# The last residual add moved from the vector engine into accumulating transfers to the output

## The reference, cut to what matters

```python
def sandwich_update(x, y_mix, mod, g, w1, w2):
    x = x + mod[2] * rmsnorm(y_mix, g[1])
    h = modulate(rmsnorm(x, g[2]), mod[3], mod[4])
    return x + mod[5] * rmsnorm(sq_relu_mlp(h, w1, w2), g[3])
```

## Time and profile before

| what | value |
| --- | --- |
| median of 3 runs | 1409.69 us (1409.33 to 2283.79) |
| the profiled execution's own time | 1409.05 us |
| its span, first to last instruction | 1407.0 us |
| PE busy | 1365.7 us (97%) |
| DVE busy | 889.8 us (63%) |
| ACT busy | 607.8 us (43%) |
| POOL busy | 123.1 us (9%) |
| DRAM read, written | 164.49 MB, 10.49 MB |

### The profile page before, as it was taken

One profiled execution on the slowest core, in us unless ns is written; L12 is line 12 of the kernel. 1 busy time (PEld: TensorE's weight loads), 2 busy tenths in 40 slices (PEclk: granted clock), 3 DMA queues, 4 the chain that ended last, 5 costly groups with the idle time before them and its releaser, 6 DMA issues. The chain is left out here.

```text
span 1407.0 us, 18116 instructions
## 1 busy us (share of the span) xinstructions
PE 1365.7 (97%) x6676; PEld 1123.4 (80%) x6676; DVE 889.8 (63%) x1279; ACT 607.8 (43%) x903; POOL 123.1 (9%) x151
## 2 busy tenths in 40 slices
PE   9989998999999999999998999999999999999996
PEld 2568787988888888888878888888888888888885
DVE  6898779977765555555457799998274333333333
ACT  3655446664462432514445344434446143251441
POOL 1761120002000000000110000000200000000011
PEclk9999999999999999999999999999999999999997
DMA  9534251119266565665221232230303233233221
GB/s 360 219 147 170 82 169 47 46 46 326 78 214 205 182 208 179 198 202 174 97 90 61 75 105 71 95 120 31 120 31 113 97 94 101 92 102 103 91 75 60
DMA packets 48331, 178.47 MB, mean 127 GB/s; under 512 B 5929, under 2 KB 6249, under 8 KB 45835
## 3 DMA queue, kind: packets, MB, share of 16 engines
q1 hardware_dynamic: 45194, 164.51, 34.4%
q0 software_dynamic: 3072, 13.11, 2.9%
HBM read 164.49 MB, written 10.49 MB: 124 GB/s over the span
## 5 line engine op out<-in xcount | busy, mean ns | idle before, releaser
L1758 PE MATMUL bank<-hhi,whi 128*128 128x512 f32 (+1 forms) x1000 | 377.3, 377 | 0.6 <-DVE wlo L1126 0.4
L1760 PE MATMUL bank<-hhi,wlo 128*128 128x512 f32 (+1 forms) x1000 | 374.4, 374 | 0.0
L1759 PE MATMUL bank<-hlo,whi 128*128 128x512 f32 (+1 forms) x1000 | 374.4, 374 | 0.0
L695 ACT ACTIVATE whi<-raw 128x1024 fp32r<-128x1024 f32 x180 | 189.1, 1053 | 231.6 <-PE bank L1760 199.9
L1126 DVE TENSOR_TENSOR wlo<-raw,whi 128x1024 fp32r<-128x1024 f32 x180 | 222.4, 1237 | 92.7 <-ACT whi L695 91.1
L1758 PEld LDWEIGHTS bank<-hhi,whi 128*128 128x128 f32 x1000 | 188.7, 189 | 34.4 <-issue 1.4
L1760 PEld LDWEIGHTS bank<-hhi,wlo 128*128 128x128 f32 x1000 | 188.6, 189 | 34.0
L1759 PEld LDWEIGHTS bank<-hlo,whi 128*128 128x128 f32 x1000 | 188.7, 189 | 32.8
L1760 PE MATMUL bank<-ghi,wlo 128*128 128x512 f32 x512 | 199.2, 389 | 0.0
L1758 PE MATMUL bank<-ghi,whi 128*128 128x512 f32 x512 | 199.2, 389 | 0.0
L1759 PE MATMUL bank<-glo,whi 128*128 128x512 f32 x512 | 199.2, 389 | 0.0
(11 more groups left out here) (275 smaller groups left out, 1963.8 us busy)
## 6 DMA issues: line engine op xcount, KB each, us to landing
raw<-in_wpack SPq DMA_DIRECT2D x180, 512.0 KB, 3.5
araw<-in_apack SPq DMA_DIRECT2D x40, 512.0 KB, 3.5
amore<-in_apack SPq DMA_DIRECT2D x36, 512.0 KB, 3.5
ablk<-in_ahead SPq DMA_DIRECT2D x8, 1024.0 KB, 12.3
spectra<-scratch SPq DMA_DIRECT2D x16, 512.0 KB, 2.9
araw<-spectra POOLq DMA_DIRECT2D x8, 1024.0 KB, 5.1
fs<-in_fw SPq DMA_DIRECT2D x2, 1024.0 KB, 11.2
x<-in_xT SPq DMA_DIRECT2D x1, 2048.0 KB, 14.6
```

The costliest lines, as they stand in the source:

```text
L695: A(whi[:, s, :], raw[:, r, :], ACT.Copy).then_inc(hi_done, 1)
L1758: mm(o, lh, rh, start=first, stop=False)
L1759: mm(o, lh, rl, start=False, stop=False)
L1760: return mm(o, ll, rh, start=False, stop=last)
```

## The change

Boundary 3 on DVE loses its four additions and keeps the four multiplications. SP writes the eight blocks of `x` to the output during the last MLP, between two weight loads, under a new semaphore `x_base`. POOL, after its last sum of squares, waits for `x_base`, then for each `scaled_done`, and issues two transfers a group from `y` to the output that add to what lies there (`accum_op=ALU.add`). SP's last waits are for both semaphores.

```diff
@@ -573,11 +574,12 @@
             load_quarter(QUARTERS - 1, ADA_ROWS - ADA_RING - ADA_OUT - (QUARTERS - 1) * ADA_QUARTER)
-            load_units(U_HY + 5, UNITS)
-            for i in range(X_GROUPS):
-                sp.wait_ge(x_done, 3 * X_GROUPS + i + 1)
-                for j in range(2 * i, 2 * i + 2):
-                    sp.dma_start(out[j], x[:, j, :]).then_inc(x_out, 16)
+            load_units(U_HY + 5, UNITS - 6)
+            sp.wait_ge(x_done, 3 * X_GROUPS)
+            for j in range(KC):
+                sp.dma_start(out[j], x[:, j, :]).then_inc(x_base, 16)
+            load_units(UNITS - 6, UNITS)
+            sp.wait_ge(x_base, KC * 16)
             for n in range(2):
                 sp.wait_ge(filt_out[n], 8 * 16)
             sp.wait_ge(x_out, KC * 16)
@@ -680,6 +682,11 @@
             y_sums(2)
             y_sums(3)
+            pool.wait_ge(x_base, KC * 16)
+            for i in range(X_GROUPS):
+                pool.wait_ge(scaled_done, 3 * X_GROUPS + i + 1)
+                for j in range(2 * i, 2 * i + 2):
+                    pool.dma_start(out[j], y[:, j, :], accum_op=ALU.add).then_inc(x_out, 16)
 
@@ -1497,8 +1504,6 @@
                         rows = B3[:, :].unsqueeze(1).broadcast_to([P, 2, NT])
                         TT(y[:, js, :], y[:, js, :], rows, ALU.mult).then_inc(scaled_done, 1)
-                        dve.wait_ge(scaled_done, X_GROUPS * b + i + 1)
-                        TT(x[:, js, :], x[:, js, :], y[:, js, :], ALU.add).then_inc(x_done, 1)
                     return
```

More of the change, by code:

```diff
@@ L203, in build @@
         x_out = sem("x_out")
+        x_base = sem("x_base")
         hi_done = sem("hi_done")
```

## The result

The changed kernel takes 1416.55 us (median of 6 runs, 1415.39 to 1417.19). Its ratio to the kernel before is 1.0046, 95% interval 1.0036 to 1.0056: slower by 6.5 us, 5 to 8. That is far inside the 2% that were called no change, and clear all the same. The one run of before at 2283.79 us is not in the ratio. The forecast was 1411, with a range of 1404 to 1428.

A forecast was written before the change was run, and what follows sets the result against it. The end was taken as bound by DVE, then one landing. Dropping four additions gains 5.0 us, but adding transfers at half the copy rate lose 6.6, net +1.6 over the profiled 1409.05; as a median 1411, range 1404 to 1428.

The forecast's parts named there:

- narrower range of the mechanism that was forecast: Whole kernel: time 1408 to 1416 from varied data start, read rate and issue cost; the forecast mechanism had chance 0.37.
- sign for giving the forecast up: End of the span: the forecast falls if it moves by more than 7 us.
- The loss: Whole kernel: net 1.6 us over the profiled time, from 5.0 us gained on DVE and 6.6 us lost in transfers.
- DVE's 5.0 us: Boundary 3 on DVE: without its four additions it ends 5.0 us earlier, at 1398.8 instead of 1403.81.
- The rate of adding: Final output transfers: adding fetches two operands per byte stored, so 4.19 MB at 385 GB/s take 10.9 us.
- The stretch of the data: Final adding transfers: data move from 1396.8 for 10.9 us, until 1407.7.
- The end behind the last byte: End of the kernel: the span ends 0.9 us after the last data, at 1408.6.
- SP's writes at zero: Early writes of x between loads 173 and 174: eight issues take 3.1 us in a 5.5 us gap, cost zero.
- adding as cheap as copying: Final transfers: adding costs no more than copying, data end at 1402.2, time 1405.2 profiled, 1405.8 as median; chance 0.22.
- Rows one after another: Final transfers: each row fetched, added and stored before the next, 86 us in series, time 1486; chance 0.09.
- DVE holding POOL's issues off: End of boundary 3: POOL cannot issue until DVE's multiplications end at 1398.8, time 1414; chance 0.03.
- The rival of 1.5 to 3 us a transfer: Final transfers: each adding one costs 1.5 to 3 us in listing or moving, time 1412 to 1424; chance 0.27.

The follow-up runs named there:

- e6_merged: Changed kernel with one adding transfer of 512 KB for each group instead of two of 256 KB; 1415.74 us, ratio 1.0047 to the kernel before.
- e2_pool_out: Kernel before with its last eight plain output transfers issued by POOL instead of SP; 1413.08 us, ratio 1.0014.
- e7_pool_last: Kernel before plus one 128 x 1 POOL multiplication behind DVE's last addition, which nobody waits for; 1411.6 us, ratio 1.0014.
- e1_copy: Changed kernel with its eight adding transfers turned into plain copies, so the output lacks x; 1410.02 us, ratio 0.9997 to the kernel before.
- e5_pool_adds: Kernel before, but POOL's own tensor_tensor adds groups 0 and 1 and DVE only groups 2 and 3; 1408.38 us, ratio 0.9988.
- e8_pool_three: Kernel before, but POOL's own arithmetic adds chunks 0 to 2 during DVE's scalings and DVE adds the rest; 1409.21 us, ratio 0.9992.
- e4_one_group: Changed kernel with adding transfers for group 0 only; DVE adds and SP writes groups 1 to 3; 1408.94 us, ratio 0.9994 to the kernel before.
- e9_mix: Kernel before, but group 0 goes by adding transfers, POOL's arithmetic adds group 1, DVE groups 2 and 3; 1409.12 us, ratio 0.9996.
- e3_base: Kernel before plus only SP's eight early writes of x between the loads of units 173 and 174; 1410.18 us, ratio 0.9998.

## Why the prediction was right, and where it was not

The direction was right and the range of 1404 to 1428 held the time. But the narrower range of the mechanism that was forecast, 1408 to 1416, did not hold the median of 1416.55. The wide range reached that far because of a rival whose mechanism is not there, so that it held the time is in part luck. The sign for giving the forecast up, an end of the span moved by more than 7 us, was missed narrowly: it moved by 6.6. The loss was put at 1.6 us against the profiled time and was 6.3 (1415.39 - 1409.05). By its steps:

- **DVE's 5.0 us**: right. Scalings 1.14 us apart, DVE done at 1399.0 against 1398.8, and 0.24 us of that is the shift ahead.
- **The rate of adding**: right, and it was the heart of the sum. 192 GB/s was taken, half of copying; the windows show about 200 once the stretch is under way, and swapping the adding for copying gives 6.8 us back. The Trainium skill, "Collectives: The Full Stack", section "The bandwidth ceiling: the fold count and why AG ≠ RS ≠ AR", has a reduction between cores move at half the rate of a copy. This trace agrees for an adding transfer on one core: 178 ns for an adding row of 2 KB, 172 ns for 4 KB of a copy.
- **The stretch of the data**: mis-sized. The sum had full rate from 1396.8 to the last byte. In fact the first issue came 0.55 us after POOL was released, each list took 0.89 us instead of 0.53, and the last byte was moved at 1410.45 instead of 1407.7, which is 2.5 us late when the shift is taken off. Against 192 GB/s, bytes worth 1.3 us are lacking by 1399 (the windows of 33 and 100 GB/s), 0.6 more from 1399 to 1402, and 0.8 at the end, where the engines' share falls to 0.59 and 0.12; the full rate in between makes 0.2 good. e6_merged shows that the lists as such are not the pace: with shorter lists the landing comes only 0.5 us sooner. What slows the first rows, and why the engines end unevenly, stays open.
- **The end behind the last byte**: this is the step that failed. The sum took the 0.9 us of before from the earlier trace rows as a constant. It is 3.2 us, and e2_pool_out and e7_pool_last show why: POOL closes its program 4.5 us or more after its last work, and 2.3 us or more after its last landing. Before, POOL had been idle since 1386, and that it was idle was listed only as a readiness, never as a cover that the change takes away.
- **SP's writes at zero**: right, though SP's issues cost 5.4 us and not 3.1.
- **The rivals**: adding as cheap as copying is refuted by e1_copy. Rows one after another is refuted by the rate. DVE holding POOL's issues off did not happen: they started 0.54 us apart throughout the scalings. The rival of 1.5 to 3 us a transfer would give this time, and its mechanism is not there: a list takes 0.89 us and does not set the pace, and to move a transfer takes about 1.3 us (0.26 MB at 200 GB/s).

Together: 2.5 us in the data and 2.3 behind the last byte, plus the shift of 0.2, less 0.3 because span and time lay 1.8 us apart in this execution and not 2.05. That makes 4.7, the difference between 1.6 and 6.3.

## What to carry to other kernels

An addition moved into the transfers is not free: where the engines are already full, it doubles the time of the bytes, and it belongs in a stretch with time to spare, never behind the last instruction. Ask of each engine what it does in the last 5 us: an engine that has long been idle has closed its program in cover, and any work given to it there, however small, brings that close to the end. And when the end is bound by one engine, another engine's own arithmetic can take part of its work: POOL's additions gave the only gain whose interval keeps clear of zero (1.7 us, 0.4 to 3.0). That this is more than adding transfers for one group can give (0.8 us, -0.4 to 2.1) is not shown, as the intervals overlap.

## What the runs showed of the hardware

- POOL's program is closed 4.5 us or more after its last instruction in all twelve executions, and 2.3 us or more after the last landing of a transfer of its own; a 0.19 us instruction at the end cost 2 us of span (e7_pool_last).
- POOL's list for an adding transfer costs 0.90 us for 128 rows and 1.26 for 256, where a plain one of 128 rows took 0.54 (e1_copy).
- POOL's and DVE's additions slow each other (2.35 to 3.33 us, 1.22 to 2.13), but POOL's addition beside DVE's scalings, which read one operand from PSUM, ran at 2.36 us, and the scalings kept their pace (4.61 us for four, as without POOL). The Trainium skill, "SBUF — State Buffer", section "Who interferes with whom", says that a DVE instruction with two inputs in SBUF (the on-chip memory that holds x and y) contends with a POOL instruction that reads there, and that one with at most one such input, outside the two-port modes, does not. e5_pool_adds and e8_pool_three agree.
- Plain issues of SP, mostly 0.33 to 0.44 us, took up to 1.04 us beside adding transfers of POOL (e4_one_group) and 1.12 just behind them (e9_mix). But they took up to 1.21 us in e3_base as well, which has no adding transfer, among its eight early writes issued one after another. So the adding transfers are not shown to be the cause; it stays open.
